# Which stage serves how many expert rows, and when TensorE adds its part

## The chip, the cores and the metric

The kernel runs on one core of one Trainium2 chip. The time is device microseconds of one execution; of the kernel before, the median of 3 runs is 4076.23 us (4075.04 to 4083.37).

## What is computed

Two layers of a decoder trunk over 512 tokens of width 1024, all in float32. Cut to what matters:

```python
def _layer(x, ...):
    z = _rms(x, g_mix) @ w_in                 # one projection, cut into the branches' inputs
    y_d = _diff_attention(...)                # 4 heads, two softmaxes each
    y_m = _mla(...)                           # 8 heads, low-rank q and kv
    y_c = _short_conv(...)
    mixed = g[0] * (y_d @ w_br_diff) + g[1] * (y_m @ w_br_mla) + g[2] * (y_c @ w_br_conv)
    x = x + mixed @ w_out
    x = x + _peer(_rms(x, g_ffn), w_query, sub_keys, u_experts, v_experts)
    x = x + sigmoid(_rms(x, g_ple) @ w_ple_gate) * (p_i @ w_ple_proj)

def _peer(h, ...):                            # per token: 8 heads x 16 of 16384 experts
    expert, gate = product_key_topk(h @ w_query, sub_keys)
    act = gelu(einsum('thkd,td->thk', u_tab[expert], h))
    return einsum('thk,thkd->td', gate * act, v_tab[expert])
```

## The kernel before

**Steps.** The 512 tokens are cut in halves of 256, two tiles of 128 tokens each. With two layers that makes four steps of expert work, 0 to 3. While the experts of a half are gathered and added in step s, the same loop runs everything else of the next half: PLE of the half before (`ple_norm`, `ple_out`), then norm, convolution, projections (`qkv`, `latent`), differential attention, MLA attention, mixing (`mix_first`, `mix_more`), `out`, `ffn_norm`, `query`, `scores`, `rank` and `topk`. `stages_of` (L142) lists them. Step -1 has stages and no rows; step 3 has rows and only three stages, and step 4 closes.

**Rows.** An expert row is one of 128 experts of each token of a tile: GpSimd gathers 128 times 8 KB, u and v side by side, into one of 8 ring slots (L463). VectorE forms the dot product of u and h (`dot`, L1124). ScalarE applies gelu (L697) and multiplies by the gate (L699). The v part is added in one of two ways: VectorE adds weight times v to x (`add_row`, L1133), or ScalarE makes a diagonal matrix of the weights (L705) and TensorE multiplies it with v into the two banks of `ps_sum` (L1247), two matmuls of 512 columns. Rows with an odd number go to TensorE, even ones to VectorE. At the end of a tile VectorE adds `ps_sum` to x (L1141). A slot is free, and the next gather can start, when its v part is added (L457 to L462). There are 256 rows to a step, 1024 in all.

**Order.** Every engine works through the same plan, written by `timeline()` (L177): each stage is given `units` rows, in proportion to `COST`. ScalarE and VectorE serve the stage's rows and then do the stage's own work. TensorE holds its part of the rows back: `serve` (L1267) puts a stage's rows in `fresh`, those of the stages before in `late`. In stages with `TICKS` (the large projections) TensorE works the late rows in after the first group of matmuls and the fresh ones after later groups, two behind (`tick`, L1257). In all others it does the late rows ahead of the stage and the fresh ones in the stage behind. In the stages of `PE_FREE`, where TensorE has next to nothing to do, the fresh ones are done at once too.

**Weights** come in tiles of 1 MB over SyncE's queue into three slots: three tiles for each `ple_out` and mixing stage, two for each of `qkv`, `latent` and `out`, one for each `conv` and `query`.

## Time and profile before

| | |
|---|---|
| median of 3 runs | 4076.23 us |
| the profiled execution | 4075.65 us, its span 4073.9 us |
| TensorE busy (matmul) | 2954.1 us, 73% |
| VectorE busy | 2621.3 us, 64% |
| ScalarE busy | 1438.9 us, 35% |
| mean granted clock of TensorE | 0.84 of full |
| moved by the gathers | 1073.81 MB in 1024 gathers |
| moved over the span | 319 GB/s |

No engine is full over the span, and the memory is not either, because the stages are limited in different ways. So the profile is best read by stretch. Steps begin at about 508, 1475, 2401 and 3347 us; a step is cut into the stretches of the table below. A stage's end is the end of its last VectorE instruction, found by counting VectorE's instructions in program order. In the windows view each line is: the stretch, its length, then busy time and count of instructions of TensorE's matmuls, of its weight loads, of VectorE, ScalarE and GpSimd, then the granted clock of TensorE as a share of full, the DMA engines' busy share and GB/s. A float32 matmul stands in the records as two, so "x4" of L1247 is one row.

### The profile page before, as it was taken

Reading aid. Unit: us, or ns where it says so; the run is one execution under the profiler, and the core shown is the slowest. Engines: PE = TensorE matmul, PEld = TensorE weight load, DVE = VectorE, ACT = ScalarE, POOL = GpSimd, SP = SyncE. Lnnn points to the kernel's source line nnn. Section 1 sums busy time; section 2 is a strip of 40 time slices with the busy share of each in tenths; the row PEclk is TensorE's granted clock in tenths of the full one; section 3 lists DMA queues with packets and bytes.
Section 4 is the critical chain, followed back from the end, with each engine's and each line's share of the span. In section 5 each row is a group of like instructions: output and inputs, shape, how many; then the busy total and the mean of one; then the engine's idle time right before and its main releaser. Section 6 shows DMA issues by size and latency. Waiting matters only on the chain. (4 is left out here: it accounts for less than half of the span.)

```text
span 4073.9 us, 28650 instructions
## 1 busy us (share of the span) xinstructions
PE 2954.1 (73%) x8072; PEld 1516.8 (37%) x8072; DVE 2621.3 (64%) x5257; ACT 1438.9 (35%) x3944; POOL 1291.6 (32%) x1033
## 2 busy tenths in 40 slices
PE   8599559757998558855998558865998737556556
PEld 5354525334445225323445225333444413111112
DVE  1311676764657975684656985685556995777773
ACT  1321132656323233457333233366433223222222
POOL 0000033222333323332333333322233334555551
PEclk9689879878999779877999779977999868777778
DMA  4124279876999879987998879977899978999994
GB/s 170 47 93 144 97 318 420 307 275 230 380 404 380 322 274 379 409 323 249 386 418 361 344 271 379 420 263 264 316 421 371 399 269 353 422 422 421 422 421 185
DMA packets 182398, 1298.65 MB, mean 319 GB/s; under 512 B 20320, under 2 KB 21856, under 8 KB 26592
## 3 DMA queue, kind: packets, MB, share of 16 engines
q0 software_dynamic: 147456, 1073.81, 66.5%
q1 hardware_dynamic: 34784, 223.01, 13.7%
q8 instruction: 65, 1.06, 0.1%
q14 instruction: 93, 0.76, 0.0%
HBM read 1294.64 MB, written 2.10 MB: 318 GB/s over the span
## 5 line engine op out<-in xcount | busy, mean ns | idle before, releaser
L463 POOL DMA_INDIRECT ring<-in_uv,experts x1024 | 1289.1, 1259 | 2706.7 <-PE ps_sum L1247 1402.6
L1247 PE MATMUL ps_sum<-ring,diag 128*128 128x512 f32 x2048 | 1263.4, 753 | 777.5 <-ACT diag L705 772.8
L1124 DVE SCALAR_TENSOR_TENSOR ring<-ring,h_ffn 128x1024 f32<-128x1024 f32 x1024 | 1236.2, 1221 | 426.3 <-DMA ring<-in_uv,experts 418.6
L1247 PEld LDWEIGHTS ps_sum<-ring,diag 128*128 128x128 f32 x2048 | 441.2, 229 | 1450.8 <-ACT diag L705 1033.6
L697 ACT ACTIVATE dots<-dots 128x1 f32<-128x1 f32 x1024 | 206.2, 201 | 1734.6 <-DVE ring L1124 1733.5
L1133 DVE SCALAR_TENSOR_TENSOR x<-ring,weight,x 128x1024 f32<-128x1024 f32 x512 | 656.6, 1282 | 106.8 <-ACT weight L699 106.7
L1307 PE MATMUL ps_act<-wt,area_h 128*128 128x512 f32 (+1 forms) x1536 | 677.2, 594 | 7.7 <-ACT area_e L479 5.3
L1307 PEld LDWEIGHTS ps_act<-wt,area_h 128*128 128x128 f32 x1536 | 296.0, 193 | 372.1 <-issue 362.1
L1351 PE MATMUL ps_act<-area_h,wt 128*128 128x256 f32 x1536 | 343.6, 381 | 5.0 <-ACT area_h L479 5.0
L1351 PEld LDWEIGHTS ps_act<-area_h,wt 128*128 128x128 f32 x1536 | 292.1, 191 | 63.7 <-issue 18.4
L699 ACT ACTIVATE weight<-dots,gate 128x1 f32<-128x1 f32 x1024 | 301.6, 295 | 33.3
L1291 PE MATMUL ps_act<-ident,area_b 128*128 128x128 f32 (+1 forms) x448 | 90.7, 375 | 205.2 <-DVE area_b L762 160.1
L705 ACT ACTIVATE diag<-ident,weight 128x128 f32<-128x128 f32 x512 | 205.7, 402 | 16.8
L1486 PE MATMUL ps_dve<-wt,area_t 128*128 128x512 f32 x384 | 170.8, 592 | 0.0
L697 ACT ACT_TABLE_LOAD x125 | 160.4, 1283 | 2.2
L479 ACT ACTIVATE area_e<-ps_act 128x256 f32<-128x256 f32 (+1 forms) x160 | 71.8, 467 | 244.1 <-PE ps_act L1307 120.5
L1291 PEld LDWEIGHTS ps_act<-ident,area_b 128*128 128x128 f32 (+1 forms) x448 | 67.4, 181 | 242.3 <-DVE area_b L762 152.0
L970 DVE CUSTOM_DVE_ANT_0 area_e<-ps_dve,mask 128x128 f32<-128x128 f32 (+3 forms) x64 | 31.3, 489 | 167.0 <-PE ps_dve L1378 103.4
L493 ACT ACT_TABLE_LOAD x107 | 137.3, 1283 | 1.9
L479 ACT ACTIVATE area_b<-ps_act 128x256 f32<-128x256 f32 (+2 forms) x176 | 67.7, 407 | 160.1 <-PE ps_act L1351 98.0
L1307 PE MATMUL ps_dve<-wt,area_b 128*128 128x512 f32 x256 | 115.5, 604 | 1.9 <-ACT area_b L479 1.9
L990 DVE TENSOR_TENSOR area_f<-ps_dve,area_e 128x512 f32<-128x512 f32 x32 | 22.1, 692 | 138.8 <-PE ps_dve L1486 119.0
(173 smaller groups left out, 2108.2 us busy)
## 6 DMA issues: line engine op xcount, KB each, us to landing
wt<-in_weights SPq DMA_DIRECT2D x192, 1024.0 KB, 9.0
ring<-in_uv,experts POOLq DMA_INDIRECT x1024, 11.2
wt<-in_weights SPq DMA_DIRECT2D x12, 512.0 KB, 8.5
wt<-in_weights SPq DMA_DIRECT2D x4, 768.0 KB, 8.3
x<-in_x SPq DMA_DIRECT2D x4, 512.0 KB, 5.2
area_y<-in_keys SPq DMA_DIRECT2D x4, 512.0 KB, 10.0
area_f<-in_keys SPq DMA_DIRECT2D x4, 512.0 KB, 11.7
area_f<-in_ffn_rows SPq DMA_DIRECT2D x4, 512.0 KB, 7.8
```

Of the source, the lines that this page charges most:

```text
L463: pool.indirect_dma_start(ring[:, row.slot, :], None, a[f"uv{row.step // 2}"][:, :], bass.IndirectOffsetOnAxis(ap=experts[:, row.step % 2, ...
L479: ins = act.activation(out, in_, func, scale=scale)
L697: act.activation(dots[:, j], dots[:, j], ACT.Gelu).then_inc(gelu_ready, 1)
L699: act.activation(weight[:, j], dots[:, j], ACT.Copy, scale=gate[:, row.step % 2, row.tile, j])\
L705: act.activation(diag[:, row.pe_before % DIAGS, :], ident[:, :], ACT.Copy, scale=weight[:, j])\
L1124: dve.scalar_tensor_tensor(u, u, 1.0, h_ffn[:, row.tile, :], ALU.mult, ALU.mult, accum_out=dots[:, row.j:row.j + 1]).then_inc(dots_ready, 1)
L1133: dve.scalar_tensor_tensor(xs, ring[:, row.slot, D:2 * D], weight[:, row.j:row.j + 1], xs, ALU.mult, ALU.add)\
L1247: ins = pe.matmul(ps_sum[:, b, :], diag[:, row.pe_before % DIAGS, :], ring[:, row.slot, D + b * 512:D + (b + 1) * 512], start=begin, stop= ...
L1291: ins = pe.transpose(b[0:s.shape[1], t * P:(t + 1) * P], s, ident[:, :])
L1307: ins = pe.matmul(banks[t][:, 0:width], lhsT[:, 4 * kh + k, t * P:(t + 1) * P], w[:, k, 0:width], start=(kh + k == 0), stop=(kh == 1 and k ...
L1351: ins = pe.matmul(b[:, 0:HALF], w[:, k, c * P:(c + 1) * P], hT[:, k, :], start=(k == 0), stop=(k == KT - 1))
L1486: ins = pe.matmul(b, (ydT, ymT, ycT)[br][:, k, t * P:(t + 1) * P], w[:, k, :], start=(k == 0), stop=(k == 3))
```

## The change

`COST` goes, and a table `ROWS_IN` takes its place. It holds, for each kind of stage, about how many rows that stage is to serve; `timeline()` still scales its sum to 256 rows per step. Rows per stretch, worked out from the two tables with the formula of `timeline()` (before, after; step 1 and step 2 are alike):

| stretch | steps 1, 2 | step 0 |
|---|---|---|
| `ple_norm`, `ple_out`, `x_norm`, conv | 38, 31 | 21, 15 |
| of these `ple_norm` / `ple_out` / `x_norm` / conv | 4, 3 / 14, 12 / 4, 4 / 16, 12 | -, - / -, - / 4, 3 / 17, 12 |
| `taps` to `latent` | 26, 21 | 26, 21 |
| `diff_turn` and differential attention | 17, 25 | 17, 24 |
| `diff_sub`, `mla_norm` to `mla_turn` | 21, 28 | 20, 28 |
| MLA attention, `mla_out` | 26, 39 | 26, 38 |
| mixing | 48, 29 | 49, 29 |
| `mix_turn`, `out`, `ffn_norm` | 17, 13 | 17, 12 |
| `query`, `scores`, `rank` | 30, 29 | 31, 28 |
| `topk` | 33, 41 | 49, 61 |

Step 3 has 16 rows in its three stages and 240 behind them, before and after.

Which rows TensorE adds is no longer `number % 2` but a list, `BY_PE`, made by `shares()` from a share per kind of stage (`PE_PART`, empty) or else `MOST`, one half. What follows from it (the counts ahead of a row, first and last row of TensorE in a tile) is looked up in `PE_BEFORE`.

`PE_FREE` becomes `ROWS_FIRST` and gains `ple_norm`, `x_norm`, `ffn_norm`, `diff_flip`, `diff_sub`, `mla_norm` and `mix_turn`: there TensorE adds the stage's own rows ahead of the stage's own work. In all stages it now also adds ahead of the stage those late or fresh rows whose slot or diagonal the stage's own rows need.

```diff
--- before.py
+++ after.py
@@ -39,7 +39,6 @@
 RING = 8
 STEP_ROWS = 2 * ROWS
 DIAGS = 4
-BY_PE = 2
 
 
 COLS = ["g_mix", "g_ple", "g_ffn", "g_dq", "g_dk", "g_dsub", "g_cq", "g_ckv", "conv"]
@@ -83,18 +82,23 @@
 
 
 
-COST = {
-    "ple_norm": 12, "ple_out": 18, "x_norm": 12, "qkv": 14, "latent": 12, "conv_c": 7, "conv_x": 7,
-    "conv_b": 7, "taps": 4, "diff_sq": 5, "diff_norm": 5, "diff_turn": 4, "diff_scores": 2, "diff_flip": 2, "diff_pv": 1,
-    "diff_sub": 5, "mla_norm": 6, "mla_up": 9, "mla_sums": 7, "mla_qk": 6, "mla_rope": 8, "mla_turn": 7, "mla_scores": 2,
-    "mla_flip": 1, "mla_pv": 1, "mla_out": 2, "mix_first": 21, "mix_more": 21, "mix_turn": 5, "out": 14,
-    "ffn_norm": 12, "query": 6, "scores": 1, "rank": 3, "topk": 6,
+ROWS_IN = {
+    "ple_norm": 4, "ple_out": 6, "x_norm": 4, "qkv": 4.5, "latent": 4, "conv_c": 2, "conv_x": 2, "conv_b": 2, "taps": 2,
+    "diff_sq": 1, "diff_norm": 1, "diff_turn": 1.5, "diff_scores": 1.2, "diff_flip": 1.2, "diff_pv": 0.6, "diff_sub": 2,
+    "mla_norm": 5, "mla_up": 5, "mla_sums": 4, "mla_qk": 3, "mla_rope": 4, "mla_turn": 4, "mla_scores": 1, "mla_flip": 0.8,
+    "mla_pv": 0.5, "mla_out": 1.5, "mix_first": 5, "mix_more": 5, "mix_turn": 2, "out": 3.5,
+    "ffn_norm": 4, "query": 1.6, "scores": 0.5, "rank": 1.6, "topk": 3,
 }
+
+
+PE_PART = {}
+MOST = 1 / 2
 
 
 TICKS = {"ple_out": 6, "conv_c": 2, "conv_x": 2, "conv_b": 2, "qkv": 4, "latent": 4, "mix_first": 6, "mix_more": 6,
          "out": 4, "query": 2}
-PE_FREE = ("taps", "diff_sq", "diff_norm", "mla_sums", "mla_qk", "mla_rope", "rank", "topk")
+ROWS_FIRST = ("ple_norm", "x_norm", "ffn_norm", "taps", "diff_sq", "diff_norm", "diff_flip", "diff_sub", "mla_norm", "mla_sums",
+              "mla_qk", "mla_rope", "mix_turn", "rank", "topk")
 
 
 class At:
@@ -182,9 +186,7 @@
         row, served, spent = [], 0, 0.0
         stages = stages_of(step)
         with_rows = 0 <= step < STEPS
-        whole = max(sum(COST[st[0]] for st in stages), 3 * STEP_ROWS)
-        if step < STEPS - 1:
-            whole = sum(COST[st[0]] for st in stages)
+        whole = sum(ROWS_IN[st[0]] for st in stages) if step < STEPS - 1 else STEP_ROWS
         for st in stages:
             at = At(tuple(base), tile)
             where[st] = at
@@ -194,7 +196,7 @@
                 tile += tiles
                 done += tiles_done(st[0], at, pairs)
                 pairs = max([n for name, n in done if name == "w_used"], default=0)
-            spent += COST[st[0]]
+            spent += ROWS_IN[st[0]]
             units = 0
             if with_rows:
                 units = int(STEP_ROWS * spent / whole + 1e-9) - served
@@ -209,6 +211,24 @@
 PLAN, WHERE, TILE_DONE = timeline()
 
 
+def shares():
+
+
+    by_pe, due = [], 0.0
+    for step, row, rest in PLAN:
+        for (name, *more), at, units in row:
+            for i in range(units):
+                due += PE_PART.get(name, MOST)
+                by_pe.append(due >= 1)
+                due -= by_pe[-1]
+        by_pe += [i % 2 == 1 for i in range(rest)]
+    return by_pe
+
+
+BY_PE = shares()
+PE_BEFORE = [sum(BY_PE[:i]) for i in range(len(BY_PE) + 1)]
+
+
 class Row:
 
 
@@ -217,11 +237,14 @@
         self.step, self.in_step = divmod(number, STEP_ROWS)
         self.tile, self.j = divmod(self.in_step, ROWS)
         self.slot, self.lap = number % RING, number // RING
-        self.by_pe = number % BY_PE == BY_PE - 1
-        self.pe_before = number // BY_PE
+        self.by_pe = BY_PE[number]
+        self.pe_before = PE_BEFORE[number]
         self.dve_before = number - self.pe_before
         self.tiles_before = number // ROWS
         self.last = self.j == ROWS - 1
+        tile_at, tile_end = number - self.j, number - self.j + ROWS
+        self.pe_first = self.pe_before == PE_BEFORE[tile_at]
+        self.pe_last = self.pe_before + 1 == PE_BEFORE[tile_end]
 
 
 class Rows:
@@ -1135,9 +1158,11 @@
 
             def add_sum():
                 row = ended.pop(0)
+                while waiting and waiting[0].number <= row.number:
+                    add_row()
                 xs = x[:, 2 * (row.step % 2) + row.tile, :]
-                dve.wait_ge(pe_rows, (row.number + 1) // BY_PE)
-                dve.wait_ge(dve_rows, row.number + 1 - (row.number + 1) // BY_PE)
+                dve.wait_ge(pe_rows, PE_BEFORE[row.number + 1])
+                dve.wait_ge(dve_rows, row.number + 1 - PE_BEFORE[row.number + 1])
                 dve.tensor_tensor(xs, ps_sum[:, :, :].rearrange("p b n -> p (b n)"), xs, ALU.add).then_inc(sum_added, 1)
 
             def serve(n, last=False):
@@ -1240,12 +1265,11 @@
             def add_row(row):
 
                 pe.wait_ge(diag_ready, row.pe_before + 1)
-                begin = row.j == BY_PE - 1
-                if begin and row.tiles_before:
+                if row.pe_first and row.tiles_before:
                     pe.wait_ge(sum_added, row.tiles_before)
                 for b in range(2):
                     ins = pe.matmul(ps_sum[:, b, :], diag[:, row.pe_before % DIAGS, :],
-                                    ring[:, row.slot, D + b * 512:D + (b + 1) * 512], start=begin, stop=row.last)
+                                    ring[:, row.slot, D + b * 512:D + (b + 1) * 512], start=row.pe_first, stop=row.pe_last)
                 ins.then_inc(pe_rows, 1)
 
             def add_rows(queue, n):
@@ -1269,13 +1293,15 @@
                 late.extend(fresh)
                 fresh[:] = rows.take(n)
                 beat[:] = [0, 0, TICKS.get(name, 1)]
-                if name in PE_FREE:
+                if name in ROWS_FIRST:
                     late.extend(fresh)
                     fresh.clear()
                 if name not in TICKS:
                     add_rows(late, len(late))
-                    needed = [row for row in fresh if row.number <= rows.next - 1 - RING]
-                    add_rows(fresh, len(needed))
+                for queue in (late, fresh):
+                    needed = [row for row in queue if row.number <= rows.next - 1 - RING
+                              or row.pe_before < PE_BEFORE[rows.next] - DIAGS]
+                    add_rows(queue, len(needed))
 
             def finish(n):
                 add_rows(late, len(late))
```

## Rows read from the trace of the kernel before

**Rows 1.** Windows view, step 1 by stretch, then the plain rows of step 3.
```profile
1474.70:1612.50 137.80, 110.62 (x353) 67.25 (x354) 78.01 (x115) 52.03 (x139) 38.99 (x35) 0.88 0.81 328
1612.50:1694.50 82.00, 73.68 (x178) 34.06 (x177) 59.77 (x85) 24.42 (x76) 32.09 (x25) 0.96 1.01 419
1694.50:1759.70 65.20, 45.61 (x135) 21.90 (x133) 46.45 (x107) 42.81 (x107) 18.83 (x20) 0.79 0.90 349
1759.70:1832.30 72.60, 40.36 (x94) 18.29 (x94) 60.17 (x96) 35.49 (x99) 26.41 (x21) 0.77 0.86 335
1832.30:1943.80 111.50, 65.33 (x193) 36.39 (x194) 54.70 (x130) 80.54 (x177) 32.94 (x27) 0.72 0.70 249
1943.80:2109.30 165.50, 165.50 (x389) 73.42 (x388) 99.99 (x142) 56.32 (x147) 54.30 (x48) 1.00 1.00 408
2109.30:2166.80 57.50, 41.63 (x108) 18.61 (x106) 34.19 (x52) 17.48 (x56) 21.05 (x16) 0.92 1.01 418
2166.80:2279.30 112.50, 99.11 (x404) 73.25 (x404) 91.54 (x319) 35.09 (x116) 38.75 (x33) 0.96 0.88 357
2279.30:2401.20 121.90, 57.91 (x68) 18.78 (x68) 117.33 (x272) 29.01 (x89) 48.65 (x34) 0.61 0.83 307
...
3411.00:4020.00 609.00, 349.18 (x484) 109.28 (x482) 441.43 (x603) 167.57 (x600) 332.61 (x235) 0.75 0.99 413
```

**Rows 2.** Groups by line, whole span: busy, mean ns of one, idle before, releasers.
```profile
L1247 PE MATMUL ps_sum<-ring,diag 128*128 128x512 f32 x2048 | 1263.4, 753 | 777.5 <-ACT diag L705 772.8 <-DVE x L1141 4.2
...
L697 ACT ACT_TABLE_LOAD x125 | 160.4, 1283 | 2.2
```

**Rows 3.** Chain that ended last, first mixing stage of step 2: start, us, what.
```profile
2897.24 1.72 PE ps_sum L1247 x4
2898.96 6.87 PE ps_act L1307 x16
```

**Rows 4.** Timeline of TensorE around the norm of `x_norm`: start us, us, idle before.
```profile
1557.23 3.56 PE L1291 MATMUL ps_act<-ident,area_b 128*128 128x128 f32 x16 [13.81 <-DVE area_b L762]
...
1564.97 3.60 PE L1247 MATMUL ps_sum<-ring,diag 128*128 128x512 f32 x8
```

**Rows 5.** Timeline of VectorE: waits in `x_norm`, ahead of `mla_sums`, in `ffn_norm`.
```profile
1549.56 1.22 DVE L1124 SCALAR_TENSOR_TENSOR ring<-ring,h_ffn 128x1024 f32<-128x1024 f32 x1 [2.78 <-DMA ring<-in_uv,experts]
...
1797.56 1.76 DVE L901 TENSOR_TENSOR area_e<-area_b 128x1536 f32<-128x1536 f32 x1 [3.76 <-ACT kept_mla_v L479]
...
3108.87 1.23 DVE L1124 SCALAR_TENSOR_TENSOR ring<-ring,h_ffn 128x1024 f32<-128x1024 f32 x1 [1.79 <-DMA ring<-in_uv,experts]
```

**Rows 6.** Timeline of VectorE in one iteration of the differential attention.
```profile
1739.68 1.22 DVE L1124 SCALAR_TENSOR_TENSOR ring<-ring,h_ffn 128x1024 f32<-128x1024 f32 x1
...
1740.82 1.22 DVE L1124 SCALAR_TENSOR_TENSOR ring<-ring,h_ffn 128x1024 f32<-128x1024 f32 x1
...
1742.54 1.28 DVE L1133 SCALAR_TENSOR_TENSOR x<-ring,weight,x 128x1024 f32<-128x1024 f32 x1 [0.49 <-ACT weight L699]
1743.74 0.74 DVE L845 SCALAR_TENSOR_TENSOR area_e<-dist,ps_dve 128x256 f32<-128x256 f32 x2
```

**Rows 7.** Timeline of TensorE in the MLA attention: three v rows running.
```profile
1867.60 3.68 PE L1247 MATMUL ps_sum<-ring,diag 128*128 128x512 f32 x4 [3.21 <-ACT diag L705]
...
1874.65 3.62 PE L1247 MATMUL ps_sum<-ring,diag 128*128 128x512 f32 x4 [2.82 <-ACT diag L705]
...
1885.10 3.52 PE L1247 MATMUL ps_sum<-ring,diag 128*128 128x512 f32 x4 [5.86 <-ACT diag L705]
```

**Rows 8.** Who waited for whom: `taps` to `latent`, then the MLA attention.
```profile
PE ps_sum L1247 <- ACT diag L705: 8.3, 2, 7.1
...
PE ps_sum L1247 <- ACT diag L705: 44.8, 12, 6.7
```

**Rows 9.** Chain that ended last, MLA attention of step 2: two v rows.
```profile
2788.01 3.78 PE ps_sum L1247 x4
...
2799.52 3.69 PE ps_sum L1247 x4
```

## The prediction

> **What bounds the kernel now.** Start with the windows view by stretch of step 1 [rows 1]; the bounds are where VectorE, counted in program order, ends one stage and begins the next. The reader is to ask of each stretch which engine has no slack, for that sets what one expert row costs there.
>
> The mixing stages (1943.8 to 2109.3) hold TensorE for 165.5 of 165.5 us at full clock; VectorE has 66 us to spare. The chain there [rows 3] is TensorE alone, branch matmuls and v rows without a gap. A v row is two matmuls (four records) and 1.72 us. As TensorE takes every second row, a row more or less in such a stretch is worth 0.86 us. The norm, PLE and conv stretch and the `taps` to `latent` stretch are alike, TensorE 80% and 90% busy, with gaps at the norms [rows 4].
>
> The top-k stretch (2279.3 to 2401.2) holds VectorE for 117.3 of 121.9 us. A dot there lasts from one start to the next 1.14 us, an add 1.20 us [rows 6], so a row costs 1.14 + 1.20/2 = 1.74 us of VectorE. Differential attention is nearly the same: its iterations run VectorE back to back [rows 6], and the 18.8 us of idle time lie mainly at its start.
>
> MLA attention (1832.3 to 1943.8) has no full engine. It is a loop: dot, gelu behind a table load, weight, diagonal, v row on TensorE, then the scores matmul behind that row, then VectorE. TensorE waited 12 times for a diagonal, 44.8 us together [rows 8], of 772.8 us over the span [rows 2]; its clock averages 0.72 of full, that is, much of the time at 1.2 GHz, and a v row takes 3.7 us [rows 9].
>
> Step 3's last 240 rows move 413 GB/s [rows 1]; they are bound by the gathers.
>
> **What is a no-op.** `PE_PART` is empty and `MOST` is 1/2, so `shares()` gives TensorE every odd row, as before; start and stop flags fall on the same matmuls. The loop added in `add_sum` finds no waiting row, since the tile's last row but one is added before. Step 3 keeps 16 rows ahead and 240 behind. The added outstanding-row conditions ask for late rows at most one tick sooner; 0 us, and at worst 1.72 us where a late row must precede a mixing stage that is TensorE-bound anyway (same work, other order).
>
> **The rows that move.** From the table of the section on the change, steps 1 and 2, each, with the price of the place:
> - `ple_norm` to `conv_b`, 38 to 31 rows. One leaves a VectorE-ordered norm, 1.74; six leave TensorE's contiguous run, 3 x 1.72 = 5.2. TensorE now does two v rows inside each of two norms, where it is idle for 13.8 us, rather than after the first matmul group behind it (the 3.6 us piece at 1564.97, 3.44 from start to start) [rows 4]: 2 x 3.4 = 6.9. Slots come free sooner, so the wait for a gather of 2.78 us in `x_norm` goes [rows 5]. Sum -16.6; bounds -7 (order and wait give nothing) and -19.
> - `taps` to `latent`, 26 to 21: -2.5 x 1.72 = -4.3, and of the 8.3 us that TensorE waits for diagonals [rows 8] I take half, as gathers are saturated there (419 GB/s). -8.3; bounds -4.3 and -12.6.
> - `diff_turn` and differential attention, 17 to 25: +8 x 1.74 = +13.9. Bounds +5 (the idle time at its start takes half) and +27 (each row 3.4, as TensorE's half-clock piece may stand in the flip).
> - `diff_sub` to `mla_turn`, 21 to 28: +7 x 1.74 = 12.2; VectorE's 3.76 us idle ahead of `mla_sums` [rows 5] is filled; one late v row ahead of `mla_up`, 3.7 at half clock, moves into the wait of `mla_norm`. +4.7; bounds 0 and +12.
> - MLA attention and `mla_out`, 26 to 39. V rows of two iterations in turn start 7.05 us apart, and 10.45 us where one iteration without a v row lies between [rows 7], so such an iteration costs 3.4 us. 12 x 7.05 and 4 x 3.4 make 98 of the 111.5 us; the rest is mostly the wait for the first scores. The change puts 18 or 19 v rows into the 16 iterations: the four bare ones fill, 4 x (7.05 - 3.4) = 14.6, and 2.5 stand second in an iteration, between 3.7 (the bare row) and 7.05 each, say 5.5: 13.8. One more row of `mla_turn` hides in the first wait, -1.7. +26.7; bounds +5 (VectorE's 57 us of slack take nearly all) and +57 (6.5 v rows at 8.8, between 7.05 and the 11.5 us of [rows 9]).
> - Mixing, 48 to 29: -9.5 x 1.72 = -16.3, one answer.
> - `mix_turn`, `out`, `ffn_norm`, 17 to 13: -1.5 x 1.72, -1.74, v rows moved into the norm -3.4, and the 1.79 us gather wait [rows 5]: -9.5; bounds -4 and -14.
> - query and rank, 30 to 29: -1.7; bounds -5 and +2, as both engines are over 80% busy.
> - top-k, 33 to 41: +8 x 1.74 = +13.9.
>
> Sum: -52.4 + 59.2 = +6.8, twice +13.6. Step 0 by the same prices: -9.5 (no PLE; 21 to 15 rows), -8.3, +12.2 (17 to 24), +6.3 (20 to 28), +24.5 (26 to 38), -17.2 (49 to 29), -10.4 (17 to 12), -5 (31 to 28), +20.9 (top-k 49 to 61): +13.5. Step 3 has the moved v rows of `ple_norm`, -3.4 or 0, as 240 gathers follow: -1.7. Together +25.4 us on the profiled execution, 4075.65 us around a span of 4073.9; it lies 0.6 under the median of 4076.23. Forecast 4101 us.
>
> What moved instruction is queued past others: in the stages added to `ROWS_FIRST` the transposes of TensorE now stand behind its wait for the last diagonal of the same stage. ScalarE makes that diagonal before the norm's squares, and VectorE's norm follows the squares, so it ends first; in `diff_flip` it can end last, which is in the bound of +27. Table loads: every interval between two exponentials of MLA already holds a row, so no switch is added; a load is 1.283 us [rows 2].
>
> **Rivals.**
> 1. Attention takes its rows into waits. For it: VectorE idles 57 us of 111.5 in MLA, TensorE 46, and DMA runs at 249 GB/s [rows 1]. Against it: the waits are of one loop that a row lengthens. Price: MLA +8 rather than +26.7, differential +9, the middle +1, so -27 per step against the forecast, 81 in three steps: 4020 us.
> 2. Each v row in attention costs the loop's full turn. Place: MLA's scores and flips. Price: 6.5 turns of 8.8 us = +57, and differential at 27: 43 per step over the sum, 4101 + 129 = 4230 at full size, 4165 at half. It decides from this point: all other terms give -20 per step, so MLA's 13 rows make the kernel slower once they cost over 1.5 us each. For it: 11.5 us between two v rows [rows 9]. Against it: iterations of 3.4 us have room for a v row.
> 3. Gathers and not TensorE bound the mixing stages. Then a row there is worth what it is worth in step 3, 609 us / 240 = 2.5 us [rows 1], and 19 rows give back 48 us instead of 16: 32 more per step, 96 in three, 4005 us. Against it: TensorE has no gap in 165.5 us, so while it is full it alone can set the time [rows 1, 3]; I leave it 0.03.
>    The Trainium skill, DMA: Bandwidth & Descriptors, section Where 436 GB/s comes from, speaks for this rival: transfers out of HBM bind near 358 GB/s per core, so these stages would be well over what memory gives. The trace disagrees with that ceiling, with 408 GB/s in mixing and 419 in the stretch of `taps` to `latent` [rows 1].
> 4. The place doesn't matter: TensorE-bound stretches give back as much as the others take, and the tables do no more than shift stage bounds. 4074 us.
>
> **How the numbers follow.** Forecast (slower by a little, own range 4085 to 4135): 0.37. Rival 1: 0.31. Rival 2: 0.14. Rival 3: 0.03. Rival 4: 0.15. A difference of 0.2%, 8 us, is about what a measurement of this kernel can tell from none. Faster 0.34, same 0.15, slower 0.51. The range takes in rival 1 with its bound (the low ends of all attention terms with half the gains' high ends, some -30 per step): 3985, and rival 2 up to a little over half its price: 4170. Outside lie some 0.07 below and 0.11 above.
>
> **What would show it.** Right: mixing 16 us shorter per step with TensorE gapless still and DMA near 330 GB/s; top-k 14 us longer with VectorE full; MLA's stretch about 138 us with some 18 waits for a diagonal; TensorE's gap ahead of a norm's transposes filled by two v rows. Wrong: MLA under 120 us (rival 1) or over 160 (rival 2); mixing shorter by more than 20 us, for then gathers and not TensorE bound it (rival 3); a TensorE wait for a diagonal that ends after VectorE's norm, for then the rows ahead cost what they were to save.

## The result and the profile after

Measured beside each other, the kernel after takes 4136.98 us (median of 4 runs, 4130.61 to 4139.37), the kernel before 4075.64 us (4 runs, 4065.74 to 4083.37). The ratio is 1.0149, 95% interval 1.0125 to 1.0174. The profiled execution of after took 4130.61 us, its span 4128.8 us, 54.9 more than the span of before.

The page's first part and its groups by line, after (the answers to [rows 2]):

```profile
PE 2996.6 (73%) x8072; PEld 1520.4 (37%) x8072; DVE 2611.9 (63%) x5257; ACT 1443.1 (35%) x3950; POOL 1307.1 (32%) x1033
...
L1271 PE MATMUL ps_sum<-ring,diag 128*128 128x512 f32 x2048 | 1304.9, 776 | 920.1 <-ACT diag L728 915.9
L1147 DVE SCALAR_TENSOR_TENSOR ring<-ring,h_ffn 128x1024 f32<-128x1024 f32 x1024 | 1231.1, 1219 | 218.6 <-DMA ring<-in_uv,experts 212.5
```

TensorE's wait for a diagonal has grown from 772.8 to 915.9 us. A v row is now L1271, a dot L1147, an add L1156, weight L722, diagonal L728. The windows view of step 1, cut as [rows 1], after:

```profile
1473.80:1595.60 121.80, 104.35 (x320) 62.47 (x321) 64.17 (x99) 45.42 (x115) 28.34 (x26) 0.89 0.81 313
1595.60:1669.40 73.80, 73.47 (x193) 36.29 (x192) 51.12 (x75) 22.78 (x70) 28.88 (x23) 1.00 0.99 400
1669.40:1763.10 93.70, 59.61 (x153) 26.78 (x152) 60.68 (x128) 51.59 (x133) 27.82 (x27) 0.74 0.88 333
1763.10:1856.40 93.30, 46.84 (x98) 19.34 (x96) 71.79 (x114) 38.59 (x108) 34.59 (x27) 0.73 0.83 323
1856.40:1980.30 123.90, 80.32 (x226) 42.14 (x227) 79.18 (x166) 89.94 (x214) 48.84 (x41) 0.79 0.86 332
1980.30:2129.10 148.80, 148.09 (x346) 65.23 (x344) 63.62 (x94) 42.91 (x97) 33.70 (x30) 1.00 0.88 337
2129.10:2181.60 52.50, 44.22 (x108) 19.43 (x108) 27.98 (x43) 15.11 (x47) 19.05 (x15) 0.97 0.92 349
2181.60:2291.30 109.70, 94.31 (x392) 69.81 (x392) 89.28 (x316) 33.93 (x113) 31.76 (x28) 0.95 0.89 347
2291.30:2422.90 131.60, 63.62 (x84) 21.50 (x84) 127.77 (x289) 34.13 (x109) 59.16 (x42) 0.71 0.89 345
```

Stretch lengths before and after, and the difference with the predicted one. Steps 0 and 2 are cut in the same way; top-k is counted from the end of `rank` to the end of VectorE's last `topk` instruction (117.6 us before in step 1; its window in [rows 1] is 4.3 us longer). The cut between `rank` and top-k stands 2 us ahead of the last VectorE instruction of `rank`, before and after alike, so it changes no difference.

| stretch | step 1 | change | predicted | steps 2 / 0 |
|---|---|---|---|---|
| norms, PLE, conv | 137.8, 121.8 | -16.0 | -16.6 | -18.0 / -11.1 |
| `taps` to `latent` | 82.0, 73.8 | -8.2 | -8.3 | -9.3 / -9.4 |
| `diff_turn`, differential attention | 65.2, 93.7 | +28.5 | +13.9 | +28.9 / +16.9 |
| `diff_sub` to `mla_turn` | 72.7, 93.3 | +20.7 | +4.7 | +20.6 / +13.1 |
| MLA attention, `mla_out` | 111.4, 123.9 | +12.5 | +26.7 | +19.2 / +18.2 |
| mixing | 165.5, 148.8 | -16.7 | -16.3 | -16.8 / -26.9 |
| `mix_turn`, `out`, `ffn_norm` | 57.5, 52.4 | -5.0 | -9.5 | -6.0 / -10.4 |
| `query`, `scores`, `rank` | 112.6, 109.8 | -2.8 | -1.7 | +1.4 / -4.9 |
| top-k | 117.6, 131.6 | +14.0 | +13.9 | +13.9 / +20.5 |

In step 1 the stretches that lean on one engine (the first two, mixing, `query` to `rank` and top-k) came out within about 1 us of their price, and mixing kept TensorE gapless (148.09 of 148.80 us) with the DMA at 337 GB/s. The loops and short stages between are off in both directions. The table is of one execution of each kernel, and a stretch moves by some us between executions: MLA attention of step 2 has the same rows and the same shares in after, e3, e4 and e9 below, and took 142.2, 137.1, 136.5 and 136.7 us.

In differential attention, the timeline of after (start us, us, idle before) shows two iterations with a v row at half clock:

```profile
1706.00 3.78 PE L1271 MATMUL ps_sum<-ring,diag 128*128 128x512 f32 x4 [4.83 <-ACT diag L728]
...
1709.57 0.42 PE L1421 MATMUL ps_act<-ident,area_e 128*128 128x128 f32 x1
...
1710.03 0.28 ACT L502 ACTIVATE area_f<-ps_act 128x128 f32<-128x128 f32 x1 [4.08 <-PE ps_act L1421]
...
1710.76 1.28 DVE L1156 SCALAR_TENSOR_TENSOR x<-ring,weight,x 128x1024 f32<-128x1024 f32 x1 [2.93 <-ACT weight L722]
...
1717.73 3.67 PE L1271 MATMUL ps_sum<-ring,diag 128*128 128x512 f32 x4 [1.58 <-ACT diag L728]
...
1721.33 0.70 PE L1402 MATMUL ps_dve<-kept_diff_kT,area_b 64*128 64x256 f32 x4
1722.16 0.75 DVE L868 SCALAR_TENSOR_TENSOR area_b<-dist,ps_dve 128x256 f32<-128x256 f32 x2 [3.14 <-PE ps_dve L1402]
```

A v row stands ahead of the flip (the transpose at 1709.57); ScalarE's copy of the flip waits 4.08 us, and behind that copy, in ScalarE's order, stand the gelu and the weight that VectorE's add waits 2.93 us for. The next one stands ahead of the scores matmul, and VectorE waits 3.14 us for the scores. In the prediction VectorE ran such iterations back to back [rows 6].

### The profile page after: what moved, and what is told of

Read it like the earlier page. It is cut to its first block, busy times and chain, and to the rows that moved or that the text cites. A ratio compares the mean times of both kernels' runs of the same rounds, so it can differ in the third digit from the quotient of the medians.

```text
span 4128.8 us, 28656 instructions
## 1 busy us (share of the span) xinstructions
PE 2996.6 (73%) x8072; PEld 1520.4 (37%) x8072; DVE 2611.9 (63%) x5257; ACT 1443.1 (35%) x3950; POOL 1307.1 (32%) x1033
## 4 chain that ended last, share of the span: by engine, by line
PE 46%; DVE 21%; ACT 12%; DMA 11%; issue 6%; POOL 1%; DVEq 0%; ACTq 0%; POOLq 0%
PE ps_act L1333 14%; PE ps_sum L1271 13%; DMA ring<-in_uv,experts 11%; PE ps_act L1377 7%; DVE ring L1147 7%; DVE x L1156 4%; PE ps_dve L1512 4%; PE ps_dve L1333 3%; ACT L720 2%; ACT area_e L516 2%; ACT L516 2%; ACT weight L722 1%; ACT diag L728 1%; POOL ring L486 1%; PE ps_dve L1377 1%
## 5 line engine op out<-in xcount | busy, mean ns | idle before, releaser
L486 POOL DMA_INDIRECT ring<-in_uv,experts x1024 | 1304.6, 1274 | 2751.4 <-PE ps_sum L1271 1327.7
L1271 PE MATMUL ps_sum<-ring,diag 128*128 128x512 f32 x2048 | 1304.9, 776 | 920.1 <-ACT diag L728 915.9
L1147 DVE SCALAR_TENSOR_TENSOR ring<-ring,h_ffn 128x1024 f32<-128x1024 f32 x1024 | 1231.1, 1219 | 218.6 <-DMA ring<-in_uv,experts 212.5
L1271 PEld LDWEIGHTS ps_sum<-ring,diag 128*128 128x128 f32 x2048 | 446.8, 235 | 1629.7 <-ACT diag L728 1224.2
L1156 DVE SCALAR_TENSOR_TENSOR x<-ring,weight,x 128x1024 f32<-128x1024 f32 x512 | 656.2, 1282 | 182.4 <-ACT weight L722 182.1
L1333 PE MATMUL ps_act<-wt,area_h 128*128 128x512 f32 (+1 forms) x1536 | 667.3, 589 | 3.4 <-ACT area_h L502 2.4
L722 ACT ACTIVATE weight<-dots,gate 128x1 f32<-128x1 f32 x1024 | 301.6, 295 | 33.3
L728 ACT ACTIVATE diag<-ident,weight 128x128 f32<-128x128 f32 x512 | 205.7, 402 | 16.7
L720 ACT ACT_TABLE_LOAD x128 | 164.2, 1283 | 2.2
L516 ACT ACT_TABLE_LOAD x110 | 141.1, 1283 | 1.9
L1333 PE MATMUL ps_dve<-wt,area_b 128*128 128x512 f32 x256 | 111.9, 594 | 1.9 <-ACT area_b L502 1.9
```

The lines of the kernel that those rows point to most:

```text
L486: pool.indirect_dma_start(ring[:, row.slot, :], None, a[f"uv{row.step // 2}"][:, :], bass.IndirectOffsetOnAxis(ap=experts[:, row.step % 2, ...
L516: act.activation(*args, **kw).then_inc(act_ops, 1)
L720: act.activation(dots[:, j], dots[:, j], ACT.Gelu).then_inc(gelu_ready, 1)
L722: act.activation(weight[:, j], dots[:, j], ACT.Copy, scale=gate[:, row.step % 2, row.tile, j])\
L728: act.activation(diag[:, row.pe_before % DIAGS, :], ident[:, :], ACT.Copy, scale=weight[:, j])\
L1147: dve.scalar_tensor_tensor(u, u, 1.0, h_ffn[:, row.tile, :], ALU.mult, ALU.mult, accum_out=dots[:, row.j:row.j + 1]).then_inc(dots_ready, 1)
```

## The experiments

Each edit is against after unless another kernel is named. "C" is differential attention with `diff_turn`, "D" `diff_sub` to `mla_turn`, "E" MLA attention; three numbers are steps 0, 1 and 2. After has C 98.2, 93.7, 107.3, D 84.7, 93.3, 92.8 and E 144.8, 123.9, 142.2 us.

### The two halves of the change

**e1_table_only**: the new table, TensorE's order as before.
```diff
-ROWS_FIRST = ("ple_norm", "x_norm", ..., "mix_turn", "rank", "topk")
+ROWS_FIRST = ("taps", "diff_sq", "diff_norm", "mla_sums", "mla_qk", "mla_rope", "rank", "topk")
```


> The change's table of rows, but TensorE's old order: it adds fresh rows ahead of a stage only in the stages of the old PE_FREE. Theory R (the rows themselves cost too much in attention, 9 more in differential attention and 8 around mla_up): differential attention and the stretch behind it stay as long as in the changed kernel (94 and 93 us in step 1), and the norms lose the order's gain of 3.4 us each: about 4150 us, slower than the changed kernel. Theory F (a v row ahead of the flip holds up TensorE, ScalarE's copy and all behind it): differential attention of step 1 falls from 94 to about 80 us, the price of 8 rows at 1.74; with the norms' loss of about 25 us, 4115 to 4130 us.

4195.98 us, ratio 1.0291 (1.0263 to 1.0318). C 102.5, 92.0, 105.9: theory F falls, and R has the direction, but the time is 46 us over its 4150. Against after, D is 16 us longer in three steps (84.7, 93.3, 92.8 there; 87.4, 100.0, 99.0 here), and the norms to conv and `query` to `rank` some 12 each.

**e2_order_only**: the new order, each stage's rows as before.
```diff
-ROWS_IN = {"ple_norm": 4, "ple_out": 6, ..., "topk": 3}
+ROWS_IN = {"ple_norm": 12, "ple_out": 18, ..., "topk": 6}   # the numbers of COST
-        whole = sum(ROWS_IN[st[0]] for st in stages) if step < STEPS - 1 else STEP_ROWS
+        whole = sum(ROWS_IN[st[0]] for st in stages) if step < STEPS - 1 else 3 * STEP_ROWS
```


> The kernel before's rows per stage (its COST table) with the changed order of TensorE alone. Theory R: the order gives 3.4 us at each of 3 norms and step, 25 to 30 us in all, and costs nothing: about 4048 us. Theory F: differential attention has only one v row in a flip in step 1 and two to three in step 0, each worth some 3 us, so a little of that goes back: 4055 us. A time above 4076 would contradict both.

4037.53 us, ratio 0.9911 (0.9888 to 0.9935). So the order alone gives 37 us, and the table alone takes 121; together they take 61, so the two are not additive. The norm, PLE and conv stretch of step 1 goes from 137.8 to 127.3 us, `query` to `rank` from 112.6 to 107.2. C stays (66.3 in step 1), and so does D (71.8).

### Is it the row ahead of the flip, the hold in `mla_up`, or its rows?

**e3_no_flip_first**: `diff_flip` taken out of `ROWS_FIRST`.

> The changed kernel, but diff_flip is taken out of ROWS_FIRST, so the v row of a flip is added after the flip. Theory F: differential attention of steps 1 and 2 falls by about 14 us each, of step 0 by 5: 4131 to 4137 less 33, 4100 us. Theory R: no change, within 5 us.

4138.11 us, ratio 1.0155; C 102.3, 91.4, 108.5, that is +4.1, -2.3 and +1.2. Putting TensorE's flip rows first, rather than behind the flip, is not the cause.

**e4_few_rows_in_up**: rows moved out of `mla_up`.
```diff
-    "mla_norm": 5, "mla_up": 5, "mla_sums": 4, "mla_qk": 3, "mla_rope": 4, "mla_turn": 4,
+    "mla_norm": 5, "mla_up": 2, "mla_sums": 4, "mla_qk": 4, "mla_rope": 5, "mla_turn": 5,
```


> The changed kernel with the same 28 rows in the stretch from diff_sub to mla_turn, but mla_up serves 2 rather than 5 (mla_qk, mla_rope and mla_turn one more each). Theory S (the v rows of mla_up wait on TensorE until after its projections, so with 4 more of mla_sums more than the 8 slots of the ring are asked for, and VectorE waits for a gather begun late: 6.3 us of DMA wait and 4.6 us for a weight in step 1): VectorE's idle time in mla_sums falls from 11 to about 4 us, 7 us per step, about 20 us in all. Theory N (the stretch is long because mla_norm's five rows stand ahead of its transposes): no change within 5 us.

4136.25 us, ratio 1.0147; D 89.9, 88.4, 88.5, that is -5 in steps 1 and 2, most of what theory S said, and +5 in step 0, and E +8 in step 0. In `mla_sums` of step 1 the wait for a gather is gone, and one of 6.10 us for a weight is left.

**e9_up_rows_midway**: TensorE adds the fresh rows of `mla_up` behind the first tile of its projections, not behind both.
```diff
+                    if t == 0:
+                        add_rows(fresh, len(fresh))
```


> The changed kernel, but TensorE adds mla_up's own v rows between the two tiles of mla_up's projections rather than behind both. Theory S (their slots are held too long, so the gathers of mla_sums start late): VectorE's idle time in mla_sums of step 1 falls from 11 to about 5 us and the stretch from diff_sub to mla_turn from 93 to 88 us, 10 to 15 us in all: 4123 us. If the hold is not the cause, the v rows stand in the way of the projections and the stretch gets 3 to 7 us longer: 4150 us.

4137.07 us, ratio 1.0146; D 87.9, 92.1, 91.6, that is +3.2, -1.2 and -1.2. The total hides two changes that cancel. Theory S is right about the gather: in after VectorE waits 4.62 us for a weight and 6.29 us for a gather in `mla_sums` of step 1 (the lines are shown further down), and here the gather's wait is gone. But TensorE's v rows now stand ahead of the second tile's projections, ScalarE's copies of those come later, and the weight stands behind the copies in ScalarE's order:

```profile
1815.02 5.31 PE L1271 MATMUL ps_sum<-ring,diag 128*128 128x512 f32 x12
...
1822.08 0.60 ACT L502 ACTIVATE area_b<-ps_act 128x512 f32<-128x512 f32 x1 [6.21 <-PE ps_act L1467]
...
1825.77 1.28 DVE L1156 SCALAR_TENSOR_TENSOR x<-ring,weight,x 128x1024 f32<-128x1024 f32 x1 [9.77 <-ACT weight L722]
```

One wait of 9.77 us takes the place of two of 10.91.

### What an expert row costs in the attentions

**e5_narrow_v**: in the attentions TensorE multiplies 64 of each 512 columns of v and leaves the rest out (but for the first and last row of a tile).
```diff
-                    ins = pe.matmul(ps_sum[:, b, :], ..., ring[:, row.slot, D + b * 512:D + (b + 1) * 512], ...)
+                    ins = pe.matmul(ps_sum[:, b, 0:n], ..., ring[:, row.slot, D + b * 512:D + b * 512 + n], ...)
```


> The changed kernel, but TensorE's matmuls for rows served in the two attentions multiply 64 of 512 columns of v per bank (the rest of those rows' v is left out). Their time falls from 3.7 to about 0.8 us at half clock. Theory L (a row's cost in attention is its turn of the loop dot, table load, gelu, weight, diagonal, v row, next matmuls, and the v row is nearly half of it): differential attention of step 1 falls from 94 to 75 us, MLA from 124 to about 100, in all some 110 to 130 us less: about 4015 us. Theory C (VectorE's and ScalarE's own in-order queues set the turn, TensorE only stands beside): under 20 us less, 4120 us.

4075.67 us, ratio 0.9994; C 96.6, 76.6, 98.1, E 132.3, 111.0, 126.7. That is 61 us less than after, about half of what theory L had promised. As the loss is 61 us too, one is led to equate the two, but before has such rows as well, and no run narrows them there.

**e6_exp_rows**: the rows' Gelu becomes Exp, so that ScalarE changes its table less often.
```diff
-act.activation(dots[:, j], dots[:, j], ACT.Gelu)
+act.activation(dots[:, j], dots[:, j], ACT.Exp)
```


> The changed kernel, but the rows apply Exp in place of Gelu, so that the attentions' Exp and the rows use one table and the two loads of 1.28 us per iteration go (the weights of the experts are other numbers). Theory L with table loads as the other large part of the turn: 2.57 us in each of 8 + 16 iterations, 20 us in differential attention and up to 40 in MLA, some 120 to 150 us in three steps: about 4000 us. If the v row alone is the turn, ScalarE waits anyway and under 40 us go.

4059.16 us, ratio 0.9956; the loads in gelu and exponentials fall from 238 to 79. C 93.8, 83.5, 99.2, E 126.0, 108.9, 116.9. The switches are worth 78 us of after; its order and table add hardly any (238 against 232 before).

**e7_attention_rows_by_dve**: VectorE adds all v parts in the attentions.
```diff
-PE_PART = {}
+PE_PART = {"diff_scores": 0, "diff_flip": 0, "diff_pv": 0, "mla_scores": 0, "mla_flip": 0, "mla_pv": 0}
```


> The changed kernel with all rows served in the two attentions added by VectorE (PE_PART 0 there), 1.20 us more of VectorE and no diagonal and no v row for every second one. Theory L: differential attention is then bound by VectorE, 61 busy + 12 x 1.2 + 10 us at its start = 86 us in step 1 (94 now), MLA 79 + 18 x 1.2 + 10 = 111 (124 now): 20 us per step less, about 4075 us. Theory C: VectorE's queue is the limit already, so its added work comes on top: 4180 us.

4050.56 us, ratio 0.9936 (0.9914 to 0.9957). C 97.7, 83.2, 98.2, E 111.9, 108.3, 112.8. Its windows of C and E in step 1:

```profile
1643.00:1726.20 83.20, 27.86 (x105) 16.92 (x103) 74.31 (x139) 48.68 (x124) 29.72 (x26) 0.58 0.96 367
...
1821.40:1929.70 108.30, 44.78 (x147) 29.72 (x148) 99.36 (x184) 82.87 (x195) 54.43 (x40) 0.55 0.93 378
```

VectorE is busy for 13.6 us more in C than in after, and the stretch is 10.5 us shorter. So a v row on TensorE costs these loops more than the add costs VectorE. e7 takes away the diagonals on ScalarE too; f2 and f3 below keep them and separate the two.

### The number of rows, or their place?

**e11_diff_rows_back**: differential attention gets its old number of rows back, mixing takes them.
```diff
-"diff_scores": 1.2, "diff_flip": 1.2, "diff_pv": 0.6,  ...  "mix_first": 5, "mix_more": 5,
+"diff_scores": 0.8, "diff_flip": 0.75, "diff_pv": 0.3,  ...  "mix_first": 6.5, "mix_more": 6.5,
```


> The changed kernel, but the 9 rows that came to differential attention go back to the mixing stages (16 and 38 rows in steps 1 and 2 instead of 25 and 29). By the price of the prediction, 1.74 us a row there and 0.86 in mixing: 8 us per step, 4113 us. By the price that the changed kernel's trace shows (28.5 us for 8 rows, 17 in step 0): 21 us in steps 1 and 2 and 10 in step 0, 4085 us.

4143.28 us, ratio 1.0164 (1.0147 to 1.0181). C 89.0, 82.4, 98.7 with 15, 16 and 16 rows, where before had 65.2 us with 17 in step 1. So 9 rows less give back 11.3 us of step 1, 1.26 us a row, and 17.2 us remain with one row less than before had. The number of rows explains the smaller part. What differs besides is which of them TensorE adds: in steps 1 and 2 of before, 5 of its 7 rows in C's loop were served in the scores stages; here 2 of 8 (after: 4 of 12).

The whole doesn't fall, because mixing takes 26 us more and MLA attention changes as well: E is 136.2, 137.6 and 154.6, that is -8.6, +13.7 and +12.4, although it serves 38, 39 and 39 rows as in after. There too the places have moved: of TensorE's rows in MLA's loop, 10 of 18 are served in the scores stages where after has 6 of 17 (step 0), and 6 of 18 where after has 10 of 18 (steps 1 and 2). Where more of them are in the scores stages, the stretch is shorter.

**f1_other_phase** (against e2): in the attentions TensorE adds the even rows, VectorE the odd ones. No stage's number of rows changes; in C's loop of steps 1 and 2 TensorE has 8 rows instead of 7, 1 instead of 5 of them in the scores stages, and in step 0 8 as before, 2 instead of 6 in the scores stages.
```diff
-                by_pe.append(due >= 1)
-                due -= by_pe[-1]
+                odd = due >= 1
+                due -= odd
+                by_pe.append(odd != (name in ("diff_scores", "diff_flip", "diff_pv", "mla_scores", "mla_flip", "mla_pv")))
```


> e2 (rows per stage of the kernel before, changed order) with TensorE taking the even rows of the attentions rather than the odd ones: no stage serves another number of rows, but of TensorE's rows in differential attention of step 1 one in eight falls in a scores stage rather than five in seven; in MLA the split hardly changes. Theory Place (a v row served in a flip or pv stage holds up flip, pv and the next scores, one served in a scores stage runs beside VectorE's work): differential attention from 66 to some 80 us, three times 14: 4080 us. Theory Count: 4037 within 8 us.

4103.55 us, ratio 1.0056 (1.0039 to 1.0073), 66 us over e2. C 98.2, 82.2, 97.5 against e2's 78.2, 66.3, 79.8: 54 of the 68 us between the two spans. Step 0, where TensorE's number of rows is the same too, has 20.0 of them. E differs by -8.5, +5.5 and +6.3. C in step 1, windows and waits (us in total, times, longest), e2:

```profile
1675.90:1742.20 66.30, 45.84 (x132) 21.49 (x130) 46.55 (x108) 43.81 (x111) 19.04 (x19) 0.77 0.89 351
...
DVE area_e L868 <- PE ps_dve L1402: 6.1, 3, 5.0
...
ACT area_f L502 <- PE ps_act L1421: 5.8, 4, 3.9
```

The same of f1 (its lines stand one further down):

```profile
1688.30:1770.40 82.10, 49.98 (x135) 23.15 (x134) 46.70 (x107) 44.43 (x112) 19.65 (x20) 0.75 0.75 290
...
DVE area_e L869 <- PE ps_dve L1403: 24.4, 6, 5.6
...
ACT area_f L503 <- PE ps_act L1422: 12.9, 6, 4.1
```

VectorE has the same work, 46.6 and 46.7 us, in 66.3 and 82.1 us; its waits for scores grow from 6.1 (and 4.6 on `area_b`) to 24.4 us.

**f2_v_in_scores** and **f3_v_in_flips** separate the places.
```diff
+PE_PART = {"diff_scores": 1, "diff_flip": 0, "diff_pv": 0, "mla_scores": 1, "mla_flip": 0, "mla_pv": 0}   # f2
+PE_PART = {"diff_scores": 0, "diff_flip": 1, "diff_pv": 0, "mla_scores": 0, "mla_flip": 1, "mla_pv": 0}   # f3
```


> The changed kernel, in the attentions all rows of the scores stages to TensorE (9 and 15 in step 1) and all others to VectorE. Theory Place: differential attention 82 us, bound by VectorE (busy 61 + 4 us more + its start), MLA about 112: near or under e7, 4040 us. Theory Count: as a line between the changed kernel (12 and 18 v rows, 94 and 124 us) and e7 (none, 83 and 108): 91 and 121 us, 4115 us.

f2: 4045.11 us, ratio 0.9919 (0.9902 to 0.9935). C 95.1, 79.2, 89.7, E 119.7, 113.4, 117.1.

> The same with the rows of the flip stages to TensorE (9 and 13 in step 1), the others to VectorE, so as many v rows as f2 in differential attention. Theory Place: differential attention 95 us or more, MLA 125 or more: 4140 us. Theory Count: as f2 within 10 us.

f3: 4205.78 us, ratio 1.0308 (1.0291 to 1.0326). C 109.7, 97.7, 111.3, E 154.9, 144.2, 156.7. The timelines show one iteration of the same content, three dots, two adds and one v row; f2:

```profile
1681.84 3.78 PE L1271 MATMUL ps_sum<-ring,diag 128*128 128x512 f32 x4 [2.17 <-ACT diag L728]
1681.94 0.74 DVE L868 SCALAR_TENSOR_TENSOR area_e<-dist,ps_dve 128x256 f32<-128x256 f32 x2
...
1685.57 0.48 PE L1421 MATMUL ps_act<-ident,area_b 128*128 128x128 f32 x1
...
1690.11 0.74 DVE L868 SCALAR_TENSOR_TENSOR area_b<-dist,ps_dve 128x256 f32<-128x256 f32 x2
```

and f3:

```profile
1741.26 0.75 DVE L868 SCALAR_TENSOR_TENSOR area_e<-dist,ps_dve 128x256 f32<-128x256 f32 x2
...
1746.24 3.78 PE L1271 MATMUL ps_sum<-ring,diag 128*128 128x512 f32 x4 [5.71 <-ACT diag L728]
...
1749.81 0.42 PE L1421 MATMUL ps_act<-ident,area_b 128*128 128x128 f32 x1
...
1750.27 0.28 ACT L502 ACTIVATE area_f<-ps_act 128x128 f32<-128x128 f32 x1 [4.08 <-PE ps_act L1421]
...
1751.00 1.28 DVE L1156 SCALAR_TENSOR_TENSOR x<-ring,weight,x 128x1024 f32<-128x1024 f32 x1 [2.68 <-ACT weight L722]
1752.20 0.75 DVE L868 SCALAR_TENSOR_TENSOR area_b<-dist,ps_dve 128x256 f32<-128x256 f32 x2
```

From scores to scores it takes 1690.11 - 1681.94 = 8.17 us in f2, VectorE without a gap, and 1752.20 - 1741.26 = 10.94 us in f3. In f2 the row of 3.78 us runs while VectorE and ScalarE do the softmax and is over when the flip is wanted. In f3 it starts where the flip is wanted, and ScalarE's copy of the flip waits 4.08 us.

**f4_v_in_flips_behind**: f3 with `diff_flip` taken out of `ROWS_FIRST`.

> f3 with diff_flip out of ROWS_FIRST, so these v rows stand behind the flip. If the order ahead of the flip is what costs: differential attention falls from f3's 95 to 82 us, three times 13: 4100 us. If the v row then holds up the pv matmul and the next scores as much: f3's time within 8 us.

4197.19 us, ratio 1.0287 (1.027 to 1.0304), C 108.3, 91.2, 109.4. All but 9 us of the loss stay. In C of step 1 ScalarE's waits for the flip fall from 30.9 us in f3 to 3.1, and VectorE's for a weight from 21.0 to 6.4, but its waits for scores grow from 4.1 to 12.4: behind the flip the row holds the next scores instead. e3 is the same edit on after, and it changed the total as little.

### Who adds the v parts, over the whole kernel

**e8_parts_by_place**: e7, and VectorE adds where TensorE is full, TensorE more where VectorE is.
```diff
+            "ple_out": 0, "conv_c": 0, "conv_x": 0, "conv_b": 0, "mix_first": 0, "mix_more": 0, "out": 0, "topk": 3 / 4}
```


> As e7, and besides VectorE adds all rows of the TensorE-bound stages (ple_out, conv, mixing, out) and TensorE three of four in top-k. By the bound of each stretch: mixing 149 to 125 us (its own matmuls alone, gathers and weights at 398 GB/s), PLE and conv 122 to 108, top-k 132 to 119, attention as in e7: 60 to 70 us per step less than the changed kernel, about 3930 us. If gathers bound the mixing stages at some 350 GB/s, mixing falls to 140 only and the time is about 3990 us.

3886.52 us, ratio 0.9534 (0.9515 to 0.9554). In step 1 mixing 128.0, top-k 119.6, norms to conv 107.1.

**e10_old_rows_with_parts**: e2 with the shares of e8.

> The kernel before's rows per stage with the changed order and the parts of e8. Theory P (the new table is right once VectorE adds the rows of TensorE's full stages, since the gathers then set mixing: 48 rows and 18 tiles at 420 GB/s are 165 us): mixing stays at 165 us, top-k falls to 108, attention by 5 to 10 us, PLE and conv by 10: about 3960 us, slower than e8's 3887. If the table doesn't matter, 3887 within 10 us.

3897.56 us, ratio 0.9564 (0.9549 to 0.958). With e8's shares the new table is worth 11 us, with intervals that overlap at the edge. In step 1 C goes from 67.4 us with 17 rows to e8's 85.3 with 25: 2.24 us per row, and 1.14 + 1.20 = 2.34 is the price of a row that VectorE dots and adds. In steps 0 and 2 it is 1.5 and 2.5 us per row (86.1 to 96.4, 83.2 to 103.2), so this price holds roughly.

**e12_more_parts**: e8, with e9's edit, and
```diff
+            "qkv": 1 / 4, "latent": 1 / 4, "topk": 1, "rank": 3 / 4,
+            "mla_norm": 3 / 4, "mla_sums": 3 / 4, "mla_qk": 3 / 4, "mla_rope": 3 / 4}
```


> e8 with TensorE adding all rows in top-k, three of four in rank and from mla_norm to mla_rope, one of four in qkv and latent, and e9's midway rows. By VectorE's load: top-k 120 to 114 us, the stretch of mla_norm 93 to 86, query and rank 110 to 105, taps to latent unchanged (gathers): 15 to 20 us per step less than e8, about 3835 us. If TensorE's half-clock v rows of 3.7 us become the limit in top-k (41 rows x 3.7 = 152), top-k gets longer, 130 to 150 us, and the time is about 3920 us.

3857.06 us, ratio 0.9466 (0.945 to 0.9483). Top-k 112.6, D 88.4 in step 1.

**f5_best_with_diff_scores** (against e12).
```diff
-PE_PART = {"diff_scores": 0,
+PE_PART = {"diff_scores": 1,
```


> e12 with one edit: in the differential attention TensorE adds the v parts of all rows served in diff_scores, VectorE those of diff_flip and diff_pv (in e12 VectorE adds all of them). Theory Place: rows that TensorE adds in the scores stages cost less than the same rows on VectorE, as f2 against e7 showed (79.2 against 83.2 us in step 1, 89.7 against 98.2 in step 2): differential attention 4 to 8 us shorter per step, the whole 3835 to 3850. Theory Count: only the number of TensorE's rows matters and e7's best was none: 3865 to 3890, differential attention longer by 5 or more per step.

3834.59 us, ratio 0.9414 (0.9393 to 0.9436), the fastest. C 90.4, 77.8, 92.7 against e12's 97.0, 83.4, 98.0. Its windows of C, E and mixing in step 1:

```profile
1558.40:1636.20 77.80, 47.86 (x144) 22.89 (x142) 63.60 (x131) 51.52 (x133) 35.56 (x27) 0.80 1.00 391
...
1724.20:1833.10 108.90, 45.65 (x147) 30.59 (x148) 99.31 (x182) 83.21 (x195) 54.50 (x40) 0.53 0.94 381
1833.10:1961.30 128.20, 126.11 (x297) 55.99 (x295) 80.26 (x108) 37.15 (x83) 43.88 (x31) 1.00 0.98 400
```

**f6_best_with_both_scores** (against f5).
```diff
-            "mla_scores": 0,
+            "mla_scores": 1 / 2,
```


> f5, and in the MLA attention TensorE adds every second v part of the rows served in mla_scores. f2 against e7 gave MLA attention 119.7, 113.4, 117.1 against 111.9, 108.3, 112.8 us with all of mla_scores' rows on TensorE. Theory Place, strictly (a scores stage hides TensorE's rows in either attention): MLA attention 3 us shorter per step or more, the whole 3825 to 3840. Theory Count (TensorE has no room in the MLA iterations, whatever the stage): MLA attention 3 to 5 us longer per step, the whole 10 to 15 us above f5.

3858.29 us, ratio 0.947 (0.945 to 0.949). E 115.8, 113.5, 121.9 against 110.8, 109.0, 112.1. In MLA even rows served in the scores stage cost more on TensorE than on VectorE. So the scores stage is the cheapest place for a v row in both loops, but only in differential attention is it better than leaving the row to VectorE; why the two loops differ in this, no run shows.

## Why the prediction was right or wrong

**Right: direction, and the prices where one engine is full.** Mixing gives back 0.88 us for each row less in steps 1 and 2 (0.86 was said), top-k takes 1.75 for each more (1.74), and the norms, PLE, conv, `taps` to `latent` stretches give what was said. The order does what was priced, at least in sum: e2 alone shows -10.5 us in the first stretch of step 1 for its 6.9 + 2.8. TensorE of after, around the norm of `x_norm`, has two v rows in what was the 13.81 us gap of [rows 4]:

```profile
1538.06 1.98 PE L1271 MATMUL ps_sum<-ring,diag 128*128 128x512 f32 x4 [2.60 <-ACT diag L728]
1541.55 1.98 PE L1271 MATMUL ps_sum<-ring,diag 128*128 128x512 f32 x4 [1.50 <-ACT diag L728]
1548.86 3.68 PE L1317 MATMUL ps_act<-ident,area_b 128*128 128x128 f32 x16 [5.33 <-DVE area_b L785]
```

The parts are not additive, though: the table alone (e1) gives 13.0 us there, the order alone 10.5, both 16.0. Rival 3 falls with mixing at -16.7 us, rival 4 with the ratio's interval.

**Wrong step: "8 x 1.74" in differential attention.** It measured +28.5, +28.9 and +16.9 where +13.9, +13.9 and +12.2 stood, 34 us over its price in three steps. The step read VectorE as back to back from one iteration [rows 6] and took that for the loop. It was back to back only because most v rows of TensorE fell in the scores stages: with the other parity the same VectorE work takes 16 us longer (f1). The table changed more than the number: with "TensorE takes odd rows", adding rows to a stage shifts which stage the odd ones fall in, from 5 of 7 in the scores stages to 4 of 12 (steps 1 and 2; in step 0 from 6 of 8 to 5 of 12). f1 shows the effect with no row moved (+54 us in C), f2 and f3 with all of after's rows (C 18.5 us apart in step 1). e11 shows that giving the rows back brings back 11.3 of the 28.5 us. So a row by itself was rather priced too high, at 1.74 against some 1.26 us (some, as e11's rows don't fall in quite the same shares), and the term that was put at nothing, where TensorE's rows fall, is the larger one, 17 us. The bound of +27, for a v row of 3.4 us standing in the flip, named the mechanism, but as a bound and not as the value, and for the flip alone; the hold of the next scores was not seen.

**Wrong step: MLA's term, in the other direction.** +26.7 stood, and +12.5, +19.2 and +18.2 was measured (in step 0 +24.5 stood); some 5 of the +19.2 are after's own execution, as the table's note says. The waits are as told:

```profile
PE ps_sum L1271 <- ACT diag L728: 42.0, 18, 5.0
```

18 waits for a diagonal, against 12 in [rows 8], but not longer in total. The turns without a v row did fill; what was over-priced is the filling: the stretch is bound by no engine, and rows that VectorE adds went into its waits (VectorE 54.70 to 79.18 us busy, idle 56.8 to 44.7). Rival 1 had that, at +8; the measured value lies between. The place has a part here too, and it fell by chance: in steps 1 and 2 the new table put 10 of TensorE's 18 rows in scores stages. With as many rows and 6 of 18 there, e11 takes 137.6 us in step 1, 26.2 over before, about the price that stood, and 31.5 over in step 2; in its step 0, with 10 of 18 there, it is 9.6 over. The prediction counted how many iterations have a v row, and not in which of their stages. Rival 2's full turn held for the differential attention, at its own price of 27, and not for MLA.

**Wrong step: `diff_sub` to `mla_turn`, +4.7 against +20.7.** VectorE's work grew by 11.6 us, as priced (12.2). The two deductions, 7.5 us of idle time that the new rows were to fill, failed: idle time grew from 12.4 to 21.5, most of it in `mla_sums` (4.0 to 11.1). In step 0, where 4 rows rather than 5 are served in `mla_up` and TensorE has 2 of them rather than 3, `mla_sums` idles 4.1 us (4.8 before). VectorE and, in front, TensorE of after there:

```profile
1806.18 7.03 PE L1271 MATMUL ps_sum<-ring,diag 128*128 128x512 f32 x16
...
1807.49 1.28 DVE L1156 SCALAR_TENSOR_TENSOR x<-ring,weight,x 128x1024 f32<-128x1024 f32 x1 [4.62 <-ACT weight L722]
...
1816.21 1.23 DVE L1147 SCALAR_TENSOR_TENSOR ring<-ring,h_ffn 128x1024 f32<-128x1024 f32 x1 [6.29 <-DMA ring<-in_uv,experts]
```

An add waits for a weight, and a dot for a gather whose slot was late. The late slot comes from TensorE's hold of `mla_up`'s rows: the wait is gone in e4 and e11 (fewer such rows) and in e9 (added earlier). The wait for the weight comes from ScalarE, which makes it behind its copies of `mla_up`'s products; before, VectorE waited 3.76 us for those copies themselves [rows 5]. More rows don't fill that wait, since their adds stand behind the same copies: it is 4.62 us here, 6.10 in e4, 6.18 in e11 and 9.77 in e9. So the deduction of 3.76 us failed, and the hold, which the prediction put at nothing, took 6.29. The other deduction, 3.7 us for the row ahead of `mla_up`, was too large: e2, with that order and the old rows, is 0.9 us shorter in D. Whose row comes first in `mla_sums` doesn't settle it: it is VectorE's in steps 1 and 2 of after, with 11 us idle, and also in step 0 of e7, f2 and f3, with 4.8. Why e4 loses 5 us in step 0 and where the rest of D's idle time (`mla_norm` idles 0.9 to 2.4 us more) comes from stays open.

**Smaller ones.** `mix_turn` to `ffn_norm` gave 5.0 instead of 9.5: of the norm's v rows less was hidden than thought. Mixing in step 0 gave 26.9 instead of 17.2. Step -1, which has no rows and was not priced, is 7 us shorter in after's profile (499.1 against 505.8 us); in e3 and e4, with the same instructions there, it takes 507.5 and 507.8, so that is a difference between executions and not the change's.

In sum C and D brought 73 us too much and MLA and mixing 39 too little, so that +54.9 stands where the prediction had +25.4. That the sum is off by only 30 us is in part luck: two errors that cancel.

## What to carry to other kernels

When two engines share an interleaved stream by "every second one", look at where in the loop the second engine's items fall before counting them: an item is cheap where its engine has nothing to hand on, and costs up to its length where a short operation that others wait for stands behind it. Whether cheap is cheaper than the other engine has to be tried loop by loop (f5 and f6). Changing the number of items per stage silently moves these places, so give the shares by stage first (250 us here, e8 against after) and tune the numbers after (11 us, e8 against e10). A price read from one iteration holds for the loop only if the other iterations have their items in the same place.
